# The post norms take spare PSUM banks, and the per-layer input projections run inside them by way of a DRAM scratch

## The reference, cut to what matters

```python
def first_block(x, ...):
    ...
    h = h + rmsnorm(m @ w_out[l], norm_mix_post[l])      # first post norm
    u2 = rmsnorm(h, norm_mlp_pre[l])
    a = jnp.square(jax.nn.relu(u2 @ w_up[l]))
    h = h + rmsnorm(a @ w_down[l], norm_mlp_post[l])     # second post norm
    return h

def second_block(...):
    for i in range(2):
        h = h + mix(rms_norm(h, attn_norm[i]))           # differential, then windowed attention
        h = h + conv_ffn(rms_norm(h, ffn_norm[i]), ...)
        gate = jax.nn.sigmoid(rms_norm(h, ple_norm[i]) @ ple_w_gate[i])
        h = h + (p[i] @ ple_w_proj[i]) * gate            # p[i]: 512 x 256, an input
    return rms_norm(h, final_norm)
```

## Time and profile before

| | us |
|---|---|
| median of 3 runs (2057.06 to 2059.71) | 2057.47 |
| profiled execution, its own time | 2060.59 |
| span of the profiled execution | 2058.8 |
| TensorE busy | 1983.8 (96%) |
| VectorE / ScalarE / GpSimd busy | 1216.3 / 889.7 / 1134.4 |
| mean granted TensorE clock | 0.986 |

### The profile page before, as it was taken

How to read it: one execution, slowest core, us unless ns; L and a number is a source line. 1 busy time by engine, 2 the same in 40 slices (tenths; PEclk the granted TensorE clock), 3 DMA queues, 4 the chain that set the end, 5 groups by cost and what they waited for, 6 DMA issues and landing times.

```text
span 2058.8 us, 25509 instructions
## 1 busy us (share of the span) xinstructions
PE 1983.8 (96%) x9428; PEld 1621.6 (79%) x9428; DVE 1216.3 (59%) x1990; ACT 889.7 (43%) x1674; POOL 1134.4 (55%) x856
## 2 busy tenths in 40 slices
PE   7999997999999899999999999999999999999997
PEld 5887886778888667777788888887787888888885
DVE  6663326333423488878675744847577675744845
ACT  4544334433333335554453443444466453443442
POOL 5345544444444376454576666555864576666553
PEclk9999998999999999999999999999999999999998
DMA  4122221223222211111223222322210223222321
GB/s 154 52 67 102 93 92 61 82 98 107 93 102 95 73 64 60 42 62 53 81 103 103 92 94 96 108 92 97 75 42 32 72 103 103 93 95 95 107 93 61
DMA packets 48653, 174.37 MB, mean 85 GB/s; under 512 B 5392, under 2 KB 5776, under 8 KB 48528
## 3 DMA queue, kind: packets, MB, share of 16 engines
q1 hardware_dynamic: 48528, 172.73, 24.5%
HBM read 170.61 MB, written 2.10 MB: 84 GB/s over the span
## 4 chain that ended last, share of the span: by engine, by line
PE 87%; DVE 10%; issue 2%; ACT 1%; DMA 0%; POOL 0%; SPq 0%; DVEq 0%; ACTq 0%; POOLq 0%
PE b L380 26%; PE b L382 25%; PE b L381 25%; PE b L402 2%; DVE ra L464 2%; PE b L394 1%; PE b L414 1%; PE b L415 1%; PE b L413 1%; PE b L432 1%; DVE h L700 1%; DVE fa L554 1%; PE b L423 1%; DVE h L656 1%; PE b L395 1%
## 5 line engine op out<-in xcount | busy, mean ns | idle before, releaser
L235 POOL TENSOR_TENSOR ra<-raw,ra 128x512 fp32r<-128x512 f32 x632 | 884.4, 1407 | 780.9 <-ACT ra L276 779.2
L380 PE MATMUL b<-ra 128*128 128x512 f32 x2528 | 1006.0, 398 | 36.8 <-DVE ra L464 23.3
L382 PE MATMUL b<-ra 128*128 128x512 f32 x2528 | 988.5, 391 | 0.0
L381 PE MATMUL b<-ra 128*128 128x512 f32 x2528 | 988.2, 391 | 0.0
L276 ACT ACTIVATE ra<-raw 128x512 fp32r<-128x512 f32 x632 | 390.4, 626 | 527.4 <-PE b L382 514.9
L380 PEld LDWEIGHTS b<-ra 128*128 128x128 f32 x2528 | 477.4, 189 | 150.2 <-issue 35.2
L382 PEld LDWEIGHTS b<-ra 128*128 128x128 f32 x2528 | 476.9, 189 | 101.7
L381 PEld LDWEIGHTS b<-ra 128*128 128x128 f32 x2528 | 478.0, 189 | 93.5
L700 DVE TENSOR_TENSOR h<-b,h 128x512 f32<-128x512 f32 x144 | 97.1, 682 | 49.7 <-PE b L382 49.1
L585 DVE TENSOR_TENSOR ra<-b,ra 128x512 fp32r<-128x512 f32 (+4 forms) x166 | 92.2, 568 | 56.8 <-ACT ra L321 37.1
L592 DVE TENSOR_TENSOR tmp<-b,rb 128x512 f32<-128x512 f32 x69 | 47.3, 690 | 127.6 <-PE b L382 127.4
(11 more groups left out here) (259 smaller groups left out, 1983.3 us busy)
## 6 DMA issues: line engine op xcount, KB each, us to landing
raw<-in_f_g SPq DMA_DIRECT2D x40, 512.0 KB, 3.5
raw<-in_f_v SPq DMA_DIRECT2D x40, 512.0 KB, 3.4
raw<-in_f_d SPq DMA_DIRECT2D x40, 512.0 KB, 3.5
raw<-in_w_up SPq DMA_DIRECT2D x32, 512.0 KB, 3.4
raw<-in_w_down SPq DMA_DIRECT2D x32, 512.0 KB, 3.5
raw<-in_p_g SPq DMA_DIRECT2D x16, 512.0 KB, 3.5
raw<-in_w_gp SPq DMA_DIRECT2D x8, 512.0 KB, 3.4
raw<-in_w_ga SPq DMA_DIRECT2D x8, 512.0 KB, 3.4
```

The source lines that it names most:

```text
L235: e.tensor_tensor(wl, src, wh.bitcast(F), ALU.subtract).then_inc(*w_low.mark(n))
L380: e.matmul(ps, wh[:, c:c + 128], xh, start=start, stop=False)
L381: e.matmul(ps, wh[:, c:c + 128], xl, start=False, stop=False)
L382: last = e.matmul(ps, wl[:, c:c + 128], xh, start=False, stop=stop)
```

## The change

Six parts. (1) `post_norm` keeps the spread in bank 7 (`keep`), so there is no `rb` copy: `residual_norm` multiplies y by bank 7 and writes into a spare bank, then multiplies by the gain and adds h, again into the spare bank. ScalarE takes the high part from that bank and copies the bank to h; VectorE takes the low part from the bank. Three spare banks rotate: `LB7[4:]` after w_out, 4 to 6 after w_down. Its rank is -2. (2) With `two`, the last of the eight squares is not added to `ssq`; TensorE sums the columns of both buffers. The squares of y are taken from the bank, before the copy. The last norm of the kernel has `two` as well. (3) The projections p_p0 and p_p1 run behind w_out and behind the last w_down, on four banks; ScalarE copies each tile to a temporary buffer and SyncE stores it to a DRAM scratch `parked`. At the start of each feed-forward part four loads of two chunks bring them into `fa`. (4) The first w_up group is copied out of its banks by ScalarE, and relu reads the copy. (5) Stages a and b of `d_o` become one product of four chunks; `s_o` is left. (6) The weights of p_p are laid out for two tiles to a unit, those of d_oa for one.

```diff
+        self.parked = nc.dram_tensor("parked", (2, 128, NC, S), F, kind="Internal").ap()
 # SyncE
+        elif kind == "park":
+            dst, src, copied, parked = a
+            w.wait_ge(*copied)
+            e.dma_start(dst, src).then_inc(*parked.mark(n, 16))
 # TensorE, columns
+            parts, free = a[0], a[1]
+            for t in free:
+                w.wait_ge(*t)
+            for k, (src, made) in enumerate(parts):
+                w.wait_ge(*made)
+                for i in range(4):
+                    x = e.matmul(m.banks[STB][:, i:i + 1], src[:, 128 * i:128 * i + 128], m.ones[:, 0:1],
+                                 start=k == 0 and i == 0, stop=k == len(parts) - 1 and i == 3,
+                                 skip_group_check=True)
 # VectorE, residual_norm
-            e.tensor_tensor(z, y, m.rb[:, :], ALU.mult).then_inc(*els.mark((n, 0)))
+            e.tensor_tensor(ps, y, banks[STB][:, :], ALU.mult).then_inc(*els.mark((n, 0)))
             w.wait_ge(els, (n, 0))
-            e.scalar_tensor_tensor(out=hk, in0=z, scalar=gain, in1=hk, op0=ALU.mult,
+            e.scalar_tensor_tensor(out=ps, in0=ps, scalar=gain, in1=hk, op0=ALU.mult,
                                    op1=ALU.add).then_inc(*els.mark(n))
...
     def square(x, src, made, then=None):
...
+        if x["left"] == 1 and x["two"]:
+            launch(root(x, (i, q, s)))
+            return
...
     def outputs(...):
-        for z, stage in enumerate("ab"):
...
+            while not ready(3):
+                yield "idle"
+            yield from linear(name + "a", 1, 4, part, 8, add, LB2)
...
+    def layer_input(l, k, free):
+        yield 0, "ac", lambda: () if len(T.free) > 4 else None
+        i, z, f = T.get()
+        t_p = load(z, A["p"][l][:, k, :], *f)
...
+    def park(l):
+        def f(j, b, tok):
+            def process():
+                yield 0, "ac", lambda: (tok,) if len(T.free) > 2 else None
+                i, z, free = T.get()
+                c = done("ac", "act", row("copy_out", z, b, tok, free))
+                bank_free[b] = (c,)
+                sig = m.sig(f"parked{l}{j}")
+                n = row("park", m.parked[l][:, j, :], z, c, sig)
+                sc.begun[n] += 3.0
+                parked[(l, j)] = (sig, n)
+                T.release(i, (sig, n))
+            launch(process())
+        return f
+
+    def layer_projection(l, lb):
+        rp = lambda k: (*hl(24 + k), pts[(l, k)]) if (l, k) in pts else None
+        yield from linear_pairs(f"p_p{l}", rp, 8, park(l), lb)
...
+            yn = norm(None, rank=-2, keep=True, two=True)
+            def parts(k, b, made):
+                uh, ul = u["slots"][k]
+                ps, g = banks[b][:, :], vc(nxt[0], nxt[1] + k)
+                yield 0, "ac", lambda: (made,)
+                done("ac", "high", row("input_high", uh, ps, g, (made,), u_free))
+                h_tok[k] = (done("ac", "act", row("copy_out", h[:, k, :], b, made, ())),)
+                launch(square(u, h[:, k, :], h_tok[k][0]))
+                yield 0, "v", lambda: h_tok[k]
+                n = row("input_low", (uh, ul), ps, g, h_tok[k][0], (made,), u_free)
+                u["tok"][k] = (done("ve", "low_v", n),)
+                bank_free[b] = (u["tok"][k][0], h_tok[k][0])
...
+        for k in range(2):
+            launch(layer_input(0, k, now("pe")))
         yield from linear("w_out4", 4, 8, rhs_m, 4, evac_y(yn), LB7)
         yield from linear("w_out1", 1, 8, rhs_m, 4, lambda j, b, t: evac_y(yn)(4 + j, b, t), LB7)
+        spare += LB7[4:]
+        yield from layer_projection(0, LB7[:4])
...
+                    if blk == 0:
+                        yield 0, "ac", lambda: (tok,) if len(T.free) > 1 else None
+                        i, z, free = T.get()
+                        c = done("ac", "act", row("copy_out", z, b, tok, free))
+                        bank_free[b] = (c,)
+                        yield 0, "v", lambda: (c, u2["rb"]) if u2["rb"] else None
+                        v = done("ve", "evac", row("relu", z, z, u2["rb"], (), c))
...
             if blk == 6:
+                for k in range(2):
+                    launch(layer_input(1, k, a_free[-1]))
...
+        yield from layer_projection(1, [0, 1, 2, 3])
         return u3
 # the feed-forward part of the second block
-        for k in range(2):
-            launch(inputs_p(k))
+        launch(fetch())
...
+        def fetch():
+            yield 0, "ac", lambda: heads_end
+            for j in range(0, NC, 2):
+                pl[j] = pl[j + 1] = load(fa[:, j:j + 2, :], m.parked[l][:, j:j + 2, :], *heads_end, parked[(l, j)],
+                                         parked[(l, j + 1)])
...
-        yield from linear(f"p_p{l}", 4, 2, rp, 8, evac_pp, LB7)
```

More of the change, by code:

```diff
@@ L648, in vector_program @@
         elif kind == "residual_norm":
-            z, y, hk, gain, rb, y_done, free = a
+            b, y, hk, gain, rb, y_done, free = a
+            ps = banks[b][:, :]
             w.wait_ge(*rb)
@@ L1035, in spread, with norm, square @@
         return done("pe", "stat_t", n)
-    def norm(slots, sums=None, rank=-3):
-        return dict(slots=slots, tok=[None] * NC, n=0, sum=None, rb=None, spread=None, last=False, sums=sums, rank=rank)
+    def norm(slots, sums=None, rank=-3, keep=False, two=False):
+        return dict(slots=slots, tok=[None] * NC, n=0, sum=None, rb=None, spread=None, last=False, sums=sums, rank=rank, keep=keep, two=two)
     def rhs_of(x):
         return lambda k: (*x["slots"][k], x["tok"][k]) if x["tok"][k] else None
-    def square(x, src, made):
+    def square(x, src, made, then=None):
         yield 0, "ac", lambda: (made,) if x["n"] == 0 or (x["sum"] and T.free) else None
@@ L1049, in square @@
             x["left"] = NC - 1
+            if then:
+                then(x["sum"])
             return
@@ L1149, in build, with outputs @@
     obk = 6
-    def outputs(name, part, ready, scores_done, evac):
+    def outputs(name, part, ready, scores_done, evac, early):
         def add(j, b, tok):
             h_tok[j] = bank_free[b] = (done("ve", "evac", row("residual", h[:, j, :], banks[b][:, :], (tok,), h_tok[j])),)
-        for z, stage in enumerate("ab"):
-            while not ready(2 * z + 1):
+        if early:
+            for z, stage in enumerate("ab"):
+                while not ready(2 * z + 1):
+                    yield "idle"
+                yield from linear_pairs(name + stage, lambda k: part(2 * z + k), 8, add, LB2)
+        else:
+            while not ready(3):
                 yield "idle"
-            yield from linear_pairs(name + stage, lambda k: part(2 * z + k), 8, add, LB2)
+            yield from linear(name + "a", 1, 4, part, 8, add, LB2)
         while not ready(5) or not scores_done():
@@ L1617, in first_block, with post_norm @@
         rhs_m = lambda k: (*hl(MM[k]), m_tok[k]) if k in m_tok else None
-        def post_norm(gain, nxt, u_free):
-            yn = norm(None)
+        def post_norm(gain, nxt, u_free, spare):
+            yn = norm(None, rank=-2, keep=True, two=True)
             u = norm(U_A, rank=-2 if nxt[0] == "attn" else -3)
-            def residual(k):
[L1625 to L1632, removed]
+            def parts(k, b, made):
[9 more added lines that the diff above has]
+                bank_free[b] = (u["tok"][k][0], h_tok[k][0])
+            def residual(k):
+                yield 0, "v", lambda: (yn["rb"], y_tok[k], *bank_free[spare[0]]) if yn["rb"] and (
+                    bank_free[spare[0]] is not None) and (k < 2 or u["tok"][k - 2]) else None
+                b = rot(spare)
+                v = done("ve", "elem_v", row("residual_norm", b, y_chunk(k), h[:, k, :], vc(gain, k), yn["rb"],
+                                             y_tok[k], bank_free[b]))
+                bank_free[b] = None
+                launch(parts(k, b, v))
                 if k + 1 < NC:
                     launch(residual(k + 1))
+                else:
+                    bank_free[STB] = (v,)
             launch(residual(0))
@@ L1655, in process @@
                 def process():
[L1656 to L1659, removed]
+                    if blk == 0:
[5 more added lines that the diff above has]
+                        v = done("ve", "evac", row("relu", z, z, u2["rb"], (), c))
+                        stat["rb_use"] = (v,)
+                    else:
+                        yield 0, "v", lambda: (tok, u2["rb"]) if u2["rb"] and len(T.free) > 1 else None
+                        i, z, free = T.get()
+                        v = done("ve", "evac", row("relu", z, banks[b][:, :], u2["rb"], free, tok))
+                        bank_free[b] = stat["rb_use"] = (v,)
                     yield 0, "ac", lambda: (v,)
@@ L1774, in ffn2 @@
         T.lend([cr, sr], *now("ve"), *now("gp"))
-        pts = {}
-        def inputs_p(k):
-            yield 0, "ac", lambda: () if 3 in a_free and len(T.free) > 4 else None
-            i, z, free = T.get()
```

(9 more changed lines are left out.)

75 lines of the change are left out of this document (41 added, 34 removed).

## The result

The changed kernel takes 2036.05 us in the median of four runs (2032.93 to 2037.8), against 2057.66 for the kernel before: a ratio of 0.9892, with an interval of 0.9874 to 0.9909. That is a gain of 21.6 us where 36.8 were forecast, and 2.05 us beyond the high end of the range. The profiled execution of after is the fastest of its four (2032.93). Set against the profiled execution of before, as the prediction's sum is, the gain is 27.7 us. On one chip the kernel before took from 2057.5 to 2067 us in 17 runs, so a few us of difference mean something only as a ratio to executions of the kernel before beside it on the same chip.

What follows compares the result with a forecast made beforehand. TensorE was taken as the bound, busy 1983.8 of 2058.8 us. Gains of 21.3 (first post norm), 13.3 (second), 1.5 (d_o) and 0.7 (end) sum to 36.8, from 2057.5 to 2020.7 us; range 2009 to 2034.

Steps and rivals of the forecast that it cites:

- Moved work: At the gate, removing the projections' 10.9 us was said to cost nothing: their cover of the gate's norm was unneeded.
- The second post norm: Pause of 12.2 us and 4.9 lost after it, shrinking to 3.0 and 0.8: gain 13.3 us.
- The first pause: Between w_out and w_up at the first post norm: 14.0 us before, 3.0 without a network step after.
- rival 1: Only moved matmuls count: pauses fill, chunks stay slow, ScalarE's static order may show; 25 us gained, 2033; chance 0.2.
- The chunks: VectorE's three operations per norm chunk take 2.1 us instead of 3.3, at 0.69 each; upper bound 1.77 per operation.
- (b): First w_up group at the first post norm: 4.6 us lost to low clock and late chunks, 0.8 left after.
- The second w_up group: After the change only the next norm's column sums and spread remain before it, 1.6 us.
- (c): Before the second w_up group, 6.9 us without network matmul: the first group holds four banks until the norm's scale.
- (d): Restarting at the second w_up group after its pause costs 1.2 us, which goes with the pause.
- d_o: Joining stages a and b saves 8 residual adds: gain 1.5 us, bounds 0 (or a loss of 2) and 4.
- Stores and fetches: The parked projections' 16 stores and 8 fetches on SyncE were costed at nothing.
- rival 4: Slower: ScalarE's projection copies wait for stores to land, starving TensorE; 43 us, 2064; chance 0.04.

Runs made afterwards that it cites:

- the turn given back: Changed kernel with its seven product banks rotated by one before the first layer's gate product (also called the rotation): ratio 0.9843 to the kernel before.
- experiments 1 and 2: First, the turn given back, 0.9843; second, the kernel before with six extra turns of the bank list before the first layer's gate, 1.0028, 5.8 us slower.
- experiment 10: The turn given back, plus each tile waiting for its own bank instead of all four of its group: ratio 0.9827 to the kernel before.
- experiment 9: The turn given back, but with the first w_up group's relu reading from the banks again: ratio 0.9889 to the kernel before.
- experiments 8 and 1: The turn given back with d_o split into its two stages again, 0.9878, and the turn given back itself, 0.9843, both against the kernel before.
- experiment 7: The turn given back, without the stores to DRAM and the fetches (output not the network's): ratio 0.9861 to the kernel before.

## Why the prediction was right or wrong

**Moved work: the step that failed.** The forecast put the removal at the gate at nothing ("That cover is not needed"). As for the cover that was right: with the turn given back the gate's row of the tally stands at 10.1 against 9.1 before. But I looked only at whether the gate's scale would be late. I did not ask what else a removed product does: it turns the list of banks. The collision it left with s_first's fixed banks costs 8.3 us from one matmul's start to the next's at the gate and slow steps after it, 5 to 8 us of the whole by the ratios of experiments 1 and 2. With the rotation the kernel has a ratio of 0.9843, 32 us below before and inside the range. The second post norm is the other large miss: its gain was put 5 us too high (below).

**The first pause (forecast 3.0, measured 5.3).** 12 of the projection's 48 matmuls stand before the column sums at 326.94, the other 36 after, so it began at 326.94 - 12 x 0.227 = 324.2; to 340.43 that is 16.2 us, less 10.9. The chain's own time was nearly right: the low part was ready at 338.3, 14.1 us behind the last w_out product, where I had 13.3 to 13.9. What I left out is that w_up takes the projection's banks and that ScalarE's copies of its last tiles queue behind the new copies of h. That is rival 1's mechanism, ScalarE's static order, at a small place (2.4 us of wait, of which experiment 10 takes 2.0).

**The chunks: right.** The operation without a row, a VectorE write of 512 columns into a bank, took what I chose, not the upper bound. VectorE's groups of the kernel after from 334 to 357 us, with GpSimd busy beside them:

```profile
L665 DVE SCALAR_TENSOR_TENSOR b<-b,vec,h 128x512 f32<-128x512 f32 x8 | 6.1, 759 | 0.3
L472 DVE SCALAR_TENSOR_TENSOR ra<-b,vec,ra 128x512 fp32r<-128x512 f32 x8 | 6.0, 744 | 0.0
L663 DVE TENSOR_TENSOR b<-fa,b 128x512 f32<-128x512 f32 x8 | 5.5, 686 | 3.0 <-PE b L440 3.0
```

Three operations are 2.19 us (forecast 2.1), none is stretched, and (b) is 0 instead of the 0.8 I left: 362.28 - 340.43 = 21.85 us for 96 matmuls, 21.8 at full pace. The Trainium skill, SBUF — State Buffer, "SBUF: two separate sides", says that a VectorE operation with two SBUF inputs and a GpSimd operation that reads SBUF exclude each other. This trace agrees: with one SBUF input there is no stretch, with two there was (1.77 in the earlier trace rows). The 62 cycles more (an estimated 65 ns) that the Trainium skill, VectorE: DVE Perf Modes, "The TRN2 errata", gives for a bank source do not show: L472 takes 744 ns from a bank, and its predecessor's shortest from SBUF in this stretch took 740.

**The second w_up group (forecast 1.6, measured 0.8 + 0.8): right**, and experiment 9 shows by which part. Alone that part is worth 5 to 9 us where (c) and (d) promised 6.9 + 1.2 - 1.6 = 6.5.

**The second post norm (forecast 13.3, tally 8.2): too high.** The projection began 15 steps before its sums at 698.20, at 694.8; to 709.88 that is 15.1 us, less 10.9 = 4.2 instead of 3.0, of which 1.26 is a wait, here for the chunk's low part. The stream after it lost nothing up to 738.83. But d_first then holds four banks and only one more is free: one further tile is computed, and the next waits 3.1 us at 742 for a bank that the next norm's scale must free. I had ended the account at 742.0, where the stretch I read ended, so the wait that was late next fell outside it.

**d_o (forecast 1.5): too small.** The ratios say 7, the tally between 750 and 1050 4.0 (experiments 8 and 1), the waits for a residual add 2.7. My upper bound was 4. Between 3 and 7 the size stays open.

**Stores and fetches cost nothing: right** (experiment 7), and with it rival 4 falls: the stores land in 2.2 to 3.2 us, and in the kernel after neither ScalarE nor VectorE has a wait that a store ended.

**The end (0.7):** the last norm's wait is now 2.5 instead of 4.37, and the tally from 1650 us on falls from 10.0 to 9.5; the step is too small to judge. Rival 1's number, 2033, was nearest, by another mechanism for the larger part. Taken together, the forecast of 36.8 stands against 32.4 by the ratio once the turn is given back. What is left is mostly the second post norm, partly made up by d_o, whose gain was put too low.

## What to carry to other kernels

A product that is moved takes its turn of every rotating resource with it: compare, before and after, which bank the last tile of a rotating product takes and which banks the next product has fixed. When a pause is filled with other work, the filler's own results must leave the banks before the waiting work can start, so let that work wait for each bank when it needs it rather than for all at once. Two changes to one pause don't add (3.0 and 8.1 us alone, 8.7 together): price the second on the pause that the first leaves. And before two part experiments are added up, take out what both of them keep.

## What the runs showed that was not expected

The engine that the profile names for a wait need not be the one that ended it: 2.40 us were put down to VectorE, whose needed operation had ended 2.1 us before the matmul started, and splitting the bank waits took them away. At the second post norm the same name, for 1.26 us, was right. After a wait of 7.9 us twelve steps took some 0.43 us each from start to start, at a granted clock of 0.50, about 2.4 us on top of the wait; with the wait at 1.1 us the clock stayed at 1.00. The cost in the whole kernel was still no more than about the wait itself (5.8 us made alone, some 8 taken away).
